# A fused two-block transformer step: one root for two norms, two projection tiles in turn, and retention in a new order

## The chip, the cores and the metric

The kernel runs on one core of one Trainium2 chip. The metric is the device time of one execution in microseconds, the median of several. All operands are float32 in HBM. The matrix products run on TensorE as three passes over split operands (below); vector work is on VectorE and ScalarE, a part of the splitting on GpSimd (POOL), and SyncE (SP) issues the DMAs.

## The reference, cut to what matters

Two blocks follow each other on 1024 tokens of width 1024. The first ends in a norm with gain g_final, the second begins with a norm with gain norm1 and a shift and scale from the condition c. A context of 256 tokens gets a norm of its own. The second block's projection has 29 tiles of 128 columns for gated linear attention and retention:

```python
def _rmsnorm(x, w):
    xf = x.astype(F32)
    y = xf * lax.rsqrt(jnp.mean(xf * xf, axis=-1, keepdims=True) + EPS)
    return (y * w).astype(x.dtype)

# end of the first block, start of the second
x  = _rmsnorm(x, g_final)
h  = _rmsnorm(x, norm1_w) * (1.0 + mod[:, 1]) + mod[:, 0]
hc = _rmsnorm(ctx, norm1_w) * (1.0 + mod_c[1]) + mod_c[0]
gq, gk, gv, gz, gg, rq, rk, rv, rg = split(h @ w_in)        # for the tokens; keys, values and gates of hc too

# retention, per head, forward and backward, chunk by chunk
scores = jnp.einsum('bhik,bhjk->bhij', qc, kc) * d_intra
o = jnp.einsum('bhij,bhjv->bhiv', scores, vc) + jnp.einsum('bhik,bhkv->bhiv', qc * q_decay, s)
s = c_decay * s + jnp.einsum('bhjk,bhjv->bhkv', kc * k_decay, vc)
o_r = _head_layernorm(o_rf + _flip(o_rb), ret_norm_w) * jax.nn.silu(rg)
```

Before this come the first block's four mixers, a feed forward and a gate; after it the output projection, a router and 16 experts.

## The kernel before

Activations lie transposed: 128 channels on the partitions, tokens along the free dimension, a tile of 8 x 1024 for the whole. Each operand of a large product is split into a high part (ScalarE, names ending in H) and a low part (VectorE or POOL, names ending in L). `gemm_steps` (line 258 on) then issues for each of 8 chunks k three matmuls, L264 to L266: high by high, low by high, high by low. The weights of tile n come into one of three buffers WR by a DMA of SP, ScalarE makes WH (L244), POOL makes WL (L252); WH and WL have two slots, and the slot of tile n is free for tile n + 2 when the last matmul of tile n is done.

The program is written by hand: for each engine there is one function that emits its instructions in order, and semaphores tie them together. `on.bank` makes the next user of a PSUM bank wait until the one before it has read it. `pe_program`, `act_program`, `dve_program`, `pool_program` and `sp_program` call the stages one after another. From the second norm to the retention, the projection of the second block (`in2_*`) is a filler: `Feed` on TensorE puts a given number of k steps between the instructions of the main stage, and notes how many units (one tile, one token segment) are then done; `Follow` on the other engines does the same units at the same point.

The second norm (`fin_*`): TensorE sums the squares over channels with a matmul by ones (`rstd_pe`, L281, banks 6 and 7; L1936, banks 4 and 5, for the squares with gain). ScalarE makes the first root as Exp(-0.5 Ln(mean + EPS)) (`rstd_act`, L293 and L298), VectorE squares it and multiplies it to the second sum (L1984, L1987), ScalarE makes the second root (L1952, L1954, once per token half), VectorE multiplies both (L1990). Then for 16 tiles of 512 tokens, 8 of the first half and 8 of the second: VectorE scales (L2004), ScalarE adds the shift and rounds to the high part (L1959), VectorE makes the low part (L1998), for which the first projection tile waits chunk by chunk. After these the squares of the context are made (L1967) and summed (L2012), one by one. A projection unit ends with a copy out of its bank: ScalarE for token segments 0 and 2 (L1880), VectorE for segment 1 (L1893), from bank 0 or 1.

Retention has four heads, h of 0 to 3, and two sets of buffers (`rmem[h % 2]`). On TensorE a head passes through: turning V (`ret_v_pe`, L2517) and K (`ret_k_pe` through `turn_pe`, L2127) to tokens on partitions, in groups of 4, 4 and 2 blocks through banks 6, 7, 6; scores (`ret_scores_pe`, L2532, banks 2 and 3); states (`ret_states_pe`, L2547); output (`ret_out_pe`, L2562 to L2564, banks 4 and 5); the root's sum (`ret_root_pe`, L281, banks 2 and 3). On VectorE: rope of K and Q (L2661, L2663, L2665), queries with decay (`ret_queries_dve`, L2736), mask on the scores (L2745), the chain of states (L2762, L2765), gate and norm (L2772, L2778, L2780). On ScalarE: decay tables (L2608, L2611), copies of V (L2133) and K (L2623, L2627), output copies (L2634, L2637), Tanh of the gate (L2642) and the root. The order in which the heads interleave is the order of the calls in `ret_pe_`, `ret_act_`, `ret_dve_` and `ret_sp`.

Of the kernel before, what the change touches and what calls it, by code (L numbers as in the profile page):

```python
# [132 lines left out]
def program(nc, I, out):  # L133
# [47 lines left out]
    def half(h):  # L181
        return slice(h * 512, h * 512 + 512)
# [1672 lines left out]

    def upto_v(*ms):

        return sum(len(s) for s in SEG[:1 + max(order2.index(m) for m in ms)])

    def in2_pe(e):  # L1860
        u = 0
        for n in range(29):
            for s, (a, b) in enumerate(SEG[n]):
                if s == 2:
                    e.wait_ge(*on("cx.lo", 7))
                e.wait_ge(*on.bank(s % 2, "in2", n, s))
                at_k = (lambda k: e.wait_ge(*on("fin.lo", s, k))) if n == 0 else None
                for _ in gemm_steps(e, N_IN2 + n, xs(S, XH2, XL2), a, b, s % 2, s == len(SEG[n]) - 1, at_k):
                    yield u
                u += 1  # L1870
                yield u

    def in2_act(e):
        for n in range(29):
            for s, (a, b) in enumerate(SEG[n]):
                if s != 1:
                    e.wait_ge(*on("gemm", N_IN2 + n, a))
                    if n >= 2:
                        e.wait_ge(*on("v", order2[n - 2]))
                    e.activation(stg2[:, n % 2 * S + a:n % 2 * S + b], bank[s % 2][:, 0:b - a], AF.Copy).then_inc(  # L1880
                        *i2_act.up("in2", n, s))
                if s == len(SEG[n]) - 1:
                    w_split_hi(e, N_IN2 + n + 2)
                yield

    def in2_dve(e):
        for n in range(29):
            for s, (a, b) in enumerate(SEG[n]):
                if s == 1:
                    e.wait_ge(*on("gemm", N_IN2 + n, a))  # L1890
                    if n >= 2:
                        e.wait_ge(*on("v", order2[n - 2]))
                    e.tensor_copy(stg2[:, n % 2 * S + a:n % 2 * S + b], bank[1][:, 0:b - a]).then_inc(  # L1893
                        *i2_dve.up("in2", n, s))
                yield

    def in2_pool(e):
        for n in range(29):
            for s in range(len(SEG[n])):
                if s == len(SEG[n]) - 1:  # L1900
                    w_split_lo(e, N_IN2 + n + 2)
                yield

    def in2_sp(e):
        for n in range(29):
            for s in range(len(SEG[n])):
                if s == len(SEG[n]) - 1:
                    w_load(e, N_IN2 + n + 3)
                    for k in range(len(SEG[n])):
                        e.wait_ge(*on("in2", n, k))  # L1910
                    size = SEG[n][-1][1]
                    e.dma_start(D_v[order2[n]][:, 0:size], stg2[:, n % 2 * S:n % 2 * S + size]).then_inc(
                        *d_v[n % 2].up("v", order2[n]))
                yield
# [16 lines left out]
    def fin_pe(e, st):  # L1931
        e.wait_ge(*on("ple.sum"))
        rstd_pe(e, acq, T, (6, 7), ("fin",))
        for h in range(2):
            e.wait_ge(*on.bank(4 + h, "fin.msq", h))
            e.matmul(bank[4 + h][:, :], ones, ac2[:, half(h)], start=True, stop=True).then_inc(*f_pe.up("fin.sum2", h))  # L1936
        st.until(2, "fin")
# [7 lines left out]

    def fin_act(e, st):
        A = f_act
        join(e, "ple")
        rstd_act(e, acq, 1024, T, (6, 7), ("fin",))
# [13 lines left out]
        for j in range(8):  # L1963
            if j > 1:
                e.wait_ge(*on("cx.add", j - 1))
# [11 lines left out]
    def fin_dve(e, st):  # L1977
# [30 lines left out]
        for j in range(1, 8):  # L2008
            e.wait_ge(*on("cx.sq", j))
            if j > 1:  # L2010
                e.wait_ge(*V.now)
# [1592 lines left out]
```

## Time and profile before

| | |
|---|---|
| time, median of 3 runs | 3753.26 us (3743.82 to 3764.45) |
| the profiled execution | 3762.52 us, span 3760.7 us |
| mean granted clock of TensorE | 0.975 |
| TensorE matmul busy | 3516.2 us (93%) |
| VectorE, ScalarE, POOL busy | 58%, 41%, 19% |
| second norm and first projection tiles | about 2162 to 2230 us of the span |
| retention | 2678.8 to 2790.8 us |
| experts | 2950 us to the end |

The span is the profiled core's time from its first instruction to its last. A share of busy time is an average over stages with different limits; what a stage is worth is read from its own waits. The granted clock is given as a share of full speed: 1.0 is 2.4 GHz and 0.5 is 1.2 GHz, and a value between is a mean over a stretch.

### The profile page before, as it was taken

To read this page: it belongs to the slowest core of one execution; us is meant where nothing else is said; L and a number is where in the kernel's file an instruction comes from. 1 tells how busy PE (TensorE), PEld (TensorE's weight loads), DVE (VectorE), ACT (ScalarE), POOL (GpSimd) and SP (SyncE) were. 2 spreads that over 40 slices of the span, in tenths; PEclk is the share of its full clock that TensorE was granted. 3 is DMA by queue.
4 is the path that set the end of the run, shared out by engine and by line. 5 is a ranking of instruction groups with operands and counts; after the bars stand their busy time and mean duration, and the time that the engine had idled before them with its cause. 6 is when DMAs were issued, how large, how long until landed. Compare 5 with 4: busy or idle time off the path is not lost. (4 is left out here: it accounts for less than half of the span.)

```text
span 3760.7 us, 45912 instructions
## 1 busy us (share of the span) xinstructions
PE 3516.2 (93%) x18441; PEld 2900.1 (77%) x18441; DVE 2170.5 (58%) x2868; ACT 1537.2 (41%) x1912; POOL 725.8 (19%) x330
## 2 busy tenths in 40 slices
PE   6999999999899999999999779999788799999996
PEld 4566777677687878888887657777666799999996
DVE  3334446545357444544425553636564899999996
ACT  3244442234212332222224342343453677766774
POOL 2111111112123122222222211111122112222210
PEclk9999999999999999999999999999989899999998
DMA  3111113143453234444311114131632899999996
GB/s 127 40 45 62 57 56 119 57 146 132 174 187 133 83 127 145 137 146 144 120 40 56 40 62 152 64 117 68 193 122 87 346 381 377 381 377 379 387 375 244
DMA packets 126692, 609.58 MB, mean 162 GB/s; under 512 B 14289, under 2 KB 15705, under 8 KB 101650
## 3 DMA queue, kind: packets, MB, share of 16 engines
q1 hardware_dynamic: 121730, 589.34, 42.8%
q0 software_dynamic: 4608, 16.78, 1.7%
q8 instruction: 148, 2.42, 0.3%
q10 hardware_dynamic: 144, 0.52, 0.0%
q14 instruction: 62, 0.51, 0.0%
HBM read 524.34 MB, written 82.22 MB: 161 GB/s over the span
## 5 line engine op out<-in xcount | busy, mean ns | idle before, releaser
L264 PE MATMUL bank<-XH,WH 128*128 128x512 f32 (+1 forms) x2568 | 1034.7, 403 | 63.7 <-DVE XL L1998 16.1
L265 PE MATMUL bank<-XL,WH 128*128 128x512 f32 (+1 forms) x2568 | 1003.9, 391 | 0.0
L266 PE MATMUL bank<-XH,WL 128*128 128x512 f32 (+1 forms) x2568 | 1001.0, 390 | 0.0
L252 POOL TENSOR_TENSOR WL<-WR,WH 128x1024 fp32r<-128x1024 f32 (+1 forms) x249 | 496.8, 1995 | 2205.5 <-ACT WH L244 2205.5
L264 PEld LDWEIGHTS bank<-XH,WH 128*128 128x128 f32 x2568 | 487.6, 190 | 211.8 <-issue 53.2
L266 PEld LDWEIGHTS bank<-XH,WL 128*128 128x128 f32 x2568 | 487.3, 190 | 105.6
L265 PEld LDWEIGHTS bank<-XL,WH 128*128 128x128 f32 x2568 | 488.5, 190 | 102.0 <-issue 6.5
L244 ACT ACTIVATE WH<-WR 128x1024 fp32r<-128x1024 f32 (+1 forms) x249 | 216.2, 869 | 598.4 <-PE bank L266 579.1
L3060 DVE TENSOR_TENSOR EL<-ER,EH 128x2816 fp32r<-128x2816 f32 x120 | 369.1, 3082 | 3.8 <-POOL warm L3303 3.8
L3055 ACT ACTIVATE EH<-ER 128x2816 fp32r<-128x2816 f32 x120 | 306.4, 2562 | 151.8 <-PE bank L3121 90.1
L3119 PE MATMUL bank<-EH,WH 128*128 128x352 f32 x1024 | 335.6, 328 | 1.5 <-DVE WL L3221 1.5
L3120 PE MATMUL bank<-EL,WH 128*128 128x352 f32 x1024 | 331.4, 324 | 0.0
L3121 PE MATMUL bank<-EH,WL 128*128 128x352 f32 x1024 | 330.9, 323 | 0.0
L264 PE MATMUL bank<-YH,WH 128*128 128x512 f32 x640 | 257.2, 402 | 19.9 <-POOL WL L252 19.9
L266 PE MATMUL bank<-YH,WL 128*128 128x512 f32 x640 | 255.0, 398 | 0.0
L265 PE MATMUL bank<-YL,WH 128*128 128x512 f32 x640 | 254.8, 398 | 0.0
L3311 POOL DMA_INDIRECT D_acc<-aq,iT x16 | 109.3, 6834 | 625.5 <-DVE aq L3235 625.5
L3129 PE MATMUL bank<-EH,HH 128*128 128x256 f32 x704 | 200.8, 285 | 0.0
L3130 PE MATMUL bank<-EL,HH 128*128 128x256 f32 x704 | 198.1, 281 | 0.0
L3131 PE MATMUL bank<-EH,HL 128*128 128x256 f32 x704 | 198.1, 281 | 0.0
L3119 PEld LDWEIGHTS bank<-EH,WH 128*128 128x128 f32 x1024 | 193.1, 189 | 1.8 <-DVE WL L3221 1.8
L3120 PEld LDWEIGHTS bank<-EL,WH 128*128 128x128 f32 x1024 | 193.3, 189 | 0.0
(516 smaller groups left out, 5051.2 us busy)
## 6 DMA issues: line engine op xcount, KB each, us to landing
ER<-in_wu_dram SPq DMA_DIRECT2D x48, 1408.0 KB, 9.1
ER<-in_wd_dram SPq DMA_DIRECT2D x40, 1408.0 KB, 10.0
aq<-in_w_ada_dram SPq DMA_DIRECT2D x96, 512.0 KB, 3.8
WR<-in_w_in_dram SPq DMA_DIRECT2D x89, 512.0 KB, 4.4
ER<-in_wg_dram SPq DMA_DIRECT2D x32, 1408.0 KB, 8.5
res<-in_wg_dram SPq DMA_DIRECT2D x16, 1408.0 KB, 8.3
res<-in_wu_dram SPq DMA_DIRECT2D x16, 1408.0 KB, 8.5
WR<-in_wg_dram SPq DMA_DIRECT2D x16, 1408.0 KB, 8.4
```

What stands on the lines that cost most here:

```text
L244: e.activation(hi, raw, AF.Copy).then_inc(*w_hi.up("w_hi", n))
L252: e.tensor_tensor(WL[:, n % 2 * 1024:n % 2 * 1024 + m], raw, hi.bitcast(F32), ALU.subtract).then_inc(*w_lo.up("w_lo", n))
L264: e.matmul(bank[bk][:, 0:b - a], whi, xhi, start=k == 0, stop=False)
L265: e.matmul(bank[bk][:, 0:b - a], whi, xlo, start=False, stop=False)
L266: mm = e.matmul(bank[bk][:, 0:b - a], wlo, xhi, start=False, stop=k == K - 1)
L3055: e.activation(eh(n), ER[n % NR], AF.Copy).then_inc(*x_act.up("e.hi", n))
L3060: e.tensor_tensor(EL[n % NR], ER[n % NR], eh(n).bitcast(F32), ALU.subtract).then_inc(*x_dve.up("e.lo", n))
L3119: e.matmul(bank[b][:, 0:QW], xh, eh(n, k * QW, k * QW + QW), start=k == 0, stop=False)
L3120: e.matmul(bank[b][:, 0:QW], xh, lo[:, k * QW:k * QW + QW], start=False, stop=False)
L3121: mm = e.matmul(bank[b][:, 0:QW], xl, eh(n, k * QW, k * QW + QW), start=False, stop=k == 7)
L3129: e.matmul(reg, hh, eh(n, k * 256, k * 256 + 256), start=k == 0, stop=False)
L3130: e.matmul(reg, hh, lo[:, k * 256:k * 256 + 256], start=False, stop=False)
```

## The change

Three parts. In the second norm, the two roots become one: with m the mean of the squares and m2 the mean of the squares with gain, the product of both roots is 1/sqrt(m2 + EPS m + EPS EPS). VectorE makes the argument from the two sums, and ScalarE takes Ln of both halves, then Exp of both halves. The first root alone, which the residual needs later, gets its Exp inside the loop over the 16 tiles. There too ScalarE makes the squares of the context, five instead of eight, and VectorE sums them afterwards in five steps.

The first two tiles of the projection are taken by token half in turn: tile 0 half 0, tile 1 half 0, tile 0 half 1, tile 1 half 1, with banks 2 and 3 for tile 1.

In retention the order of the calls changes on all four engines, K and V of heads 1 to 3 are turned through banks 2 and 3, the root's sum uses banks 4 and 5, and SP loads k2 before q2.

```diff
+    IN2_UNITS = [(n, k) for n in range(29) for k in range(len(SEG[n]))]
+    IN2_UNITS[:4] = [(0, 0), (1, 0), (0, 1), (1, 1)]
+    def in2_bank(n, s):
+        return s % 2 + 2 * (n == 1)
...
     def fin_act(e, st):
         A = f_act
         join(e, "ple")
-        rstd_act(e, acq, 1024, T, (6, 7), ("fin",))
+        e.wait_ge(*act_norm.now)
+        e.activation(warm, cn("eps"), AF.Ln).then_inc(*act_norm.up())
+        for h in range(2):
+            e.wait_ge(*on("fin", "sum", h))
+            e.activation(acq[:, half(h)], bank[6 + h][:, :], AF.Ln, scale=1.0 / 1024, bias=cn("eps")).then_inc(
+                *act_norm.up("fin", "mean", h))
         for h in range(2):
             e.wait_ge(*on("fin.msq", h))
-            e.activation(rr_[:, half(h)], rr_[:, half(h)], AF.Ln, bias=cn("eps")).then_inc(*A.up())
-            e.wait_ge(*A.now)
+            e.activation(rr_[:, half(h)], rr_[:, half(h)], AF.Ln).then_inc(*A.up("fin.ln", h))
+        for h in range(2):
+            e.wait_ge(*on("fin.ln", h))
             e.activation(rr_[:, half(h)], rr_[:, half(h)], AF.Exp, scale=-0.5).then_inc(*A.up("fin.rstd2", h))
...
+            if i in CX_SQ:
+                e.wait_ge(*on("cx"))
+                to, a, b = CX_SQ[i]
+                e.activation(to, cx[:, a:b], AF.Square).then_inc(*A.up("cx.sq", a))
+            if i in (13, 14):
+                e.wait_ge(*on("fin", "mean", i - 13))
+                e.activation(acq[:, half(i - 13)], acq[:, half(i - 13)], AF.Exp, scale=-0.5).then_inc(
+                    *act_norm.up("fin", "rstd", i - 13))
...
-            e.wait_ge(*on("fin", "rstd", h))
-            e.tensor_tensor(rq, acq[:, half(h)], acq[:, half(h)], ALU.mult).then_inc(*V.up())
+            e.wait_ge(*on("fin", "mean", h))
+            e.tensor_scalar(rq, bank[6 + h][:, :], EPS / 1024, EPS * EPS, ALU.mult, ALU.add).then_inc(*V.up())
             e.wait_ge(*on("fin.sum2", h))
             e.wait_ge(*V.now)
-            e.scalar_tensor_tensor(rq, bank[4 + h][:, :], 1.0 / 1024, rq, ALU.mult, ALU.mult).then_inc(*V.up("fin.msq", h))
-        for h in range(2):
-            e.wait_ge(*on("fin.rstd2", h))
-            e.tensor_tensor(ac2[:, half(h)], rr_[:, half(h)], acq[:, half(h)], ALU.mult).then_inc(*V.up())
+            e.scalar_tensor_tensor(rq, bank[4 + h][:, :], 1.0 / 1024, rq, ALU.mult, ALU.add).then_inc(*V.up("fin.msq", h))
...
     def ret_pe_(e):
         ret_scores_pe(e, 0)
+        ret_states_pe(e, 0)
         ret_v_pe(e, 1)
-        ret_states_pe(e, 0)
         ret_k_pe(e, 1)
-        ret_states_pe(e, 1)
         ret_out_pe(e, 0)
         ret_scores_pe(e, 1)
+        ret_states_pe(e, 1)
         ret_root_pe(e, 0)
         ret_k_pe(e, 2)
+        ret_out_pe(e, 1)
         ret_v_pe(e, 2)
-        ret_out_pe(e, 1)
+        ret_root_pe(e, 1)
...
+    def ret_turn_bank(h, c0):
+        return (2 if h else 6) + c0 // 4 % 2
```

ScalarE at the second norm, before; L1954 and L298 are Exp, L1952 and L293 Ln, L1959 the high parts:

```order
L293 ACTIVATE aq<-bank,con 128x512 x2
L298 ACT_TABLE_LOAD
L298 ACTIVATE aq<-aq 128x512 x2
L1952 ACT_TABLE_LOAD
L1952 ACTIVATE rr_<-rr_,con 128x512
L1954 ACT_TABLE_LOAD
L1954 ACTIVATE rr_<-rr_ 128x512
L1952 ACT_TABLE_LOAD
L1952 ACTIVATE rr_<-rr_,con 128x512
L1954 ACT_TABLE_LOAD
L1954 ACTIVATE rr_<-rr_ 128x512
L1959 ACTIVATE XH<-hb_,md 128x512 x16
```

The same place now; L1958 and L1962 are Ln, L1965 and L1978 Exp, L1970 the high parts, L1975 a square of the context:

```order
L1958 ACTIVATE aq<-bank,con 128x512 x2
L1962 ACTIVATE rr_<-rr_ 128x512 x2
L1965 ACT_TABLE_LOAD
L1965 ACTIVATE rr_<-rr_ 128x512 x2
L1970 ACTIVATE XH<-hb_,md 128x512 x4
L1975 ACTIVATE aq<-cx 128x512
```

Five table loads between the first Ln and the first high part have become one, and the squares stand between the high parts.

TensorE where the first half tile of the projection ends, before:

```order
L266 MATMUL bank0<-XH2,WL 128x512
L264 MATMUL bank1<-XH2,WH 128x512
L265 MATMUL bank1<-XL2,WH 128x512
L266 MATMUL bank1<-XH2,WL 128x512
L264 MATMUL bank1<-XH2,WH 128x512
```

The same place now:

```order
L266 MATMUL bank0<-XH2,WL 128x512
L264 MATMUL bank2<-XH2,WH 128x512
L265 MATMUL bank2<-XL2,WH 128x512
L266 MATMUL bank2<-XH2,WL 128x512
L264 MATMUL bank2<-XH2,WH 128x512
```

The matmuls into bank 1 (tile 0, second half) now follow those into bank 2 (tile 1, first half).

VectorE in retention, from the queries of head 0 on, before; L2661 to L2665 are a rope, L2745 the mask, L2762 and L2765 the states:

```order
L2736 TENSOR_TENSOR RM<-res,RM 128x1024 x2
L2745 SCALAR_TENSOR_TENSOR RM<-bank,RM 128x512 x2
L2661 TENSOR_TENSOR stg<-stg,res 128x1024
L2663 TENSOR_TENSOR RM<-RM,res 128x1024
L2665 TENSOR_TENSOR RM<-RM,stg 128x1024
L2661 TENSOR_TENSOR res<-res 128x1024
L2663 TENSOR_TENSOR res<-res 128x1024
L2665 TENSOR_TENSOR res<-res 128x1024
L2762 COPY RM<-bank 128x128
L2765 SCALAR_TENSOR_TENSOR RM<-RM,lg,bank 128x128 x3
L2762 COPY RM<-bank 128x128
L2765 SCALAR_TENSOR_TENSOR RM<-RM,lg,bank 128x128 x11
```

Now, behind the states of head 0 (L2798, L2801); L2695 to L2699 are a rope, L2770 queries, L2781 a mask:

```order
L2801 SCALAR_TENSOR_TENSOR RM<-RM,lg,bank 128x128 x11
L2695 TENSOR_TENSOR RM<-RM,res 128x1024
L2697 TENSOR_TENSOR RM<-RM,res 128x1024
L2699 TENSOR_TENSOR RM<-RM 128x1024
L2695 TENSOR_TENSOR res<-res 128x1024
L2697 TENSOR_TENSOR res<-res 128x1024
L2699 TENSOR_TENSOR res<-res 128x1024
L2770 TENSOR_TENSOR RM<-res,RM 128x1024 x2
L2781 SCALAR_TENSOR_TENSOR RM<-bank,RM 128x512 x2
```

The two ropes of head 2 (first K, in RM, then Q, in res) stand before the queries and the mask of head 1; before, they stood behind its mask and states.

## Rows read from the trace of the kernel before

**Rows 1.** The page, part 1: busy time, share of the span and instructions.
```profile
PE 3516.2 (93%) x18441; PEld 2900.1 (77%) x18441; DVE 2170.5 (58%) x2868; ACT 1537.2 (41%) x1912; POOL 725.8 (19%) x330
```
**Rows 2.** Waits of TensorE, 2155 to 2300: us in total, times, longest.
```profile
PE bank L264 <- DVE XL L1998: 16.1, 12, 12.2
...
PE bank L264 <- DVE stg L1893: 4.5, 1, 4.5
```
**Rows 3.** Timeline of the norm: start us, us, instruction [idle before].
```profile
2165.91 2.34 PE L1936 MATMUL bank<-aq,con 128*128 128x512 f32 x4
...
2166.15 0.69 ACT L293 ACTIVATE aq<-bank,con 128x512 f32<-128x512 f32 x1 [1.02 <-PE bank L281]
...
2169.61 0.69 DVE L1987 SCALAR_TENSOR_TENSOR rr_<-bank,rr_ 128x512 f32<-128x512 f32 x1
...
2175.32 1.28 ACT L1954 ACT_TABLE_LOAD   x1
...
2176.62 0.63 ACT L1954 ACTIVATE rr_<-rr_ 128x512 f32<-128x512 f32 x1
...
2178.01 1.41 DVE L2004 SCALAR_TENSOR_TENSOR hb_<-res,gc,aq 128x512 f32<-128x512 f32 x2
```
**Rows 4.** Timeline of the first projection tiles.
```profile
2199.79 0.50 PE L264 MATMUL bank<-XH,WH 128*128 128x512 f32 x1
...
2201.93 2.40 POOL L252 TENSOR_TENSOR WL<-WR,WH 128x1024 fp32r<-128x1024 f32 x1 [37.02 <-ACT WH L244]
...
2210.72 0.51 PE L264 MATMUL bank<-XH,WH 128*128 128x512 f32 x1 [4.46 <-DVE stg L1893]
...
2217.69 0.39 PE L266 MATMUL bank<-XH,WL 128*128 128x512 f32 x1
```
**Rows 5.** Stretches: us, busy (x) of PE, PEld, DVE, ACT, POOL, clock, DMA share.
```profile
2184.00:2200.00 16.00, 12.06 (x39) 6.04 (x38) 15.60 (x24) 8.80 (x13) 0.00 (x0) 1.00 0.00 0
...
2211.00:2214.00 3.00, 3.00 (x9) 2.26 (x9) 0.00 (x0) 0.00 (x0) 0.00 (x0) 0.53 0.82 266
...
2300.00:2500.00 200.00, 188.47 (x1231) 151.06 (x1231) 91.87 (x109) 72.41 (x93) 27.90 (x11) 0.98 0.26 93
```
**Rows 6.** Waits of TensorE in retention, 2660 to 2800.
```profile
PE bank L2127 <- DVE RM L2665: 10.1, 2, 8.2
```
**Rows 7.** Stretches of retention, columns as in rows 5.
```profile
2678.80:2783.70 104.90, 78.15 (x537) 69.06 (x535) 76.20 (x112) 53.51 (x103) 17.02 (x13) 0.87 0.37 121
...
2738.00:2746.00 8.00, 8.00 (x74) 8.00 (x74) 3.79 (x3) 5.29 (x10) 3.81 (x3) 1.00 0.17 63
```
**Rows 8.** Timeline of retention, one row for each kind of work.
```profile
2685.41 2.87 DVE L2736 TENSOR_TENSOR RM<-res,RM 128x1024 f32<-128x1024 f32 x2
...
2690.55 2.46 PE L2517 MATMUL bank<-con,RM 128*128 128x128 f32 x20
...
2729.66 2.42 ACT L2623 ACTIVATE RM<-bank,lg 128x512 f32<-128x512 f32 x4 [6.01 <-PE bank L2127]
...
2737.27 0.39 PE L2562 MATMUL bank<-RM 128*128 128x128 f32 x2
...
2742.63 4.18 PE L2547 MATMUL bank<-RM 128*128 128x128 f32 x36
...
2746.65 1.95 PE L2532 MATMUL bank<-res,RM 128*128 128x128 f32 x16
...
2747.82 1.51 DVE L2745 SCALAR_TENSOR_TENSOR RM<-bank,RM 128x512 f32<-128x512 f32 x2 [5.99 <-PE bank L2532]
...
2748.66 1.95 PE L281 MATMUL bank<-RM,con 128*128 128x512 f32 x4
...
2755.14 1.22 DVE L2661 TENSOR_TENSOR res<-res 128x1024 f32<-128x1024 f32 x1
...
2780.62 0.39 PE L2564 MATMUL bank<-RM 128*128 128x128 f32 x2
```
**Rows 9.** DMA issues of 2678 to 2740: KB each, median us to landing.
```profile
RM<-D_v SPq DMA_DIRECT2D x4, 640.0 KB, 7.6
```

More of the change, by code:

```diff
@@ L1862, in in2_pe @@
[L1862 to L1870, printed above, removed]
+        for u, (n, s) in enumerate(IN2_UNITS):
+            a, b = SEG[n][s]
+            if s == 2:
+                e.wait_ge(*on("cx.lo", 7))
+            e.wait_ge(*on.bank(in2_bank(n, s), "in2", n, s))
+            at_k = (lambda k: e.wait_ge(*on("fin.lo", s, k))) if n == 0 else None
+            for _ in gemm_steps(e, N_IN2 + n, xs(S, XH2, XL2), a, b, in2_bank(n, s), s == len(SEG[n]) - 1, at_k):
@@ L1871, in in2_pe @@
                 yield u
+            yield u + 1
     def in2_act(e):
[L1874 to L1884, printed above, removed]
@@ L1904, in in2_sp @@
-    def in2_sp(e):
[L1905 to L1914, printed above, removed]
+        for n, s in IN2_UNITS:
+            a, b = SEG[n][s]
+            if s != 1:
+                e.wait_ge(*on("gemm", N_IN2 + n, a))
+                if n >= 2:
+                    e.wait_ge(*on("v", order2[n - 2]))
+                e.activation(stg2[:, n % 2 * S + a:n % 2 * S + b], bank[in2_bank(n, s)][:, 0:b - a], AF.Copy).then_inc(
+                    *i2_act.up("in2", n, s))
+            if s == len(SEG[n]) - 1:
+                w_split_hi(e, N_IN2 + n + 2)
+            yield
@@ new lines, in in2_dve @@
+    def in2_dve(e):
+        for n, s in IN2_UNITS:
+            a, b = SEG[n][s]
+            if s == 1:
+                e.wait_ge(*on("gemm", N_IN2 + n, a))
+                if n >= 2:
+                    e.wait_ge(*on("v", order2[n - 2]))
+                e.tensor_copy(stg2[:, n % 2 * S + a:n % 2 * S + b], bank[in2_bank(n, s)][:, 0:b - a]).then_inc(
+                    *i2_dve.up("in2", n, s))
+            yield
+    def in2_pool(e):
+        for n, s in IN2_UNITS:
+            if s == len(SEG[n]) - 1:
+                w_split_lo(e, N_IN2 + n + 2)
+            yield
@@ L1936, in fin_pe @@
             e.matmul(bank[4 + h][:, :], ones, ac2[:, half(h)], start=True, stop=True).then_inc(*f_pe.up("fin.sum2", h))
+            on.bank(6 + h, "fin.msq", h)
         st.until(2, "fin")
@@ L2618, in ret_k_act @@
             e.wait_ge(*on("ret.kT", h, "T", c0))
-            b = bank[6 + c0 // 4 % 2]
+            b = bank[ret_turn_bank(h, c0)]
             for d in range(2):
```

110 lines of the change are left out of this document (60 added, 50 removed).

## The prediction, made before the changed kernel ran

> **What bounds the kernel now.** I read the busy table of the profile first: TensorE is busy 3516 of the 3760.7 us of the span [rows 1]. A change then pays only where TensorE waits, or runs at its lower clock. So I took the waits of TensorE next, stretch by stretch, for the two places that the diff touches.
>
> At the start of the second block TensorE waits 16.1 us for the low parts XL that VectorE makes, and 4.5 us for a copy out of bank 1 [rows 2], beside a shorter wait for the context's XL. The timeline shows where. The sums of squares come out of TensorE, then ScalarE and VectorE pass the ball for the two roots, and the first normalised tile starts on VectorE at 2178.01 [rows 3]. From there VectorE makes one XL with every two instructions, 24 instructions in 16 us, so one in 1.33 us [rows 5]. TensorE needs for the three matmuls that use it 0.69 us (from 2199.79 it ends the last three at 2200.5). It ends the second half of tile 0 at about 2200.5, does the first half of tile 1, stands until 2210.72 and ends tile 1 at 2218.1, 24 matmuls in 7.4 us [rows 4]. These hold a stretch at a granted clock of 0.53, the level of 1.2 GHz, right after the wait [rows 5].
>
> In the retention stage (2678.8 to 2783.7) TensorE's waits are many and small but for those on the rope of VectorE, 10.1 us with one of 8.2 [rows 6]. The mean granted clock is 0.87 there [rows 7], so some 27 us of 105 ran at 1.2 GHz, waits included (0.13 x 2 x 104.9).
>
> **The change, part A: one root.** Before, from the end of the last Ln of the first norm (2166.15 + 0.69 = 2166.84) to the first tile at 2178.01 stand 11.2 us [rows 3]. In it are five table loads of 1.28 us, of which ScalarE now needs one (the rows of its order, in the section on the change). New chain, with durations of rows 3: the square sum of half 0 leaves TensorE at about 2167.4 (second of four pieces of the row at 2165.91), that of half 1 at 2168.3. VectorE's two steps per half take 0.7 each; the first of half 0 runs at 2165.2, beside TensorE, then 2167.4 to 2168.1, then half 1 to 2169.5. Ln of half 1 ends at 2170.2, the load at 2171.5, Exp of half 0 at 2172.1. The first tile starts at 2172.2, so 5.8 us earlier. The product of the two roots (two VectorE steps) is gone as well; its only place on the chain is in these 11.2 us.
>
> The Trainium skill ("ScalarE: Activation LUTs", What ACT_TABLE_LOAD costs) charges 2.66 us for each switch, with a drain of 1.38 us. Here the load at 2175.32 takes 1.28 us and the ACTIVATE behind it starts 0.02 us after its end [rows 3], so the trace does not agree. By the page's figure four loads less would be worth 10.6 us instead of 5.1, which the 11.2 us with all their other work cannot hold.
>
> **Part B: two tiles in turn.** The steps are now tile 0 half 0, tile 1 half 0, tile 0 half 1, tile 1 half 1, in banks 0, 2, 1, 3. With D for the start on VectorE (now 2172.2): XL of half 0 is complete at D + 11.6. TensorE ends tile 0 half 0 at D + 12.3, tile 1 half 0 (8 x 0.69 = 5.5 us, nothing to wait for) at D + 17.8, tile 0 half 1 at D + 23.3 (the last XL is there at D + 22, just in time), tile 1 half 1 at D + 28.8 = 2201.0. Before, that point is 2218.1. A and B give 17.0 us; of that 5.8 is A, 5.5 the half tile that fits under VectorE's pace, 4.5 the wait for bank 1, and the rest mostly the lower clock after it.
>
> What hides the rest. The squares of the context move into ScalarE's loop: ScalarE is busy 8.8 of 16 us in that stretch [rows 5], 0.7 of each 1.33, and a square of 512 columns is an instruction like the Exp of 0.63 [rows 3], so its copies come hardly later, and VectorE has another tile to make before it wants one. VectorE's sums of the squares were 7 steps that alternated with ScalarE; now they are 5 of up to 0.7 with nothing between: 3 us, done at D + 25. The copy out of bank 1 is needed only at about D + 34. Next latest are the weights of tile 2: their slot is free at D + 23.3. Before, POOL had the low part of such a tile 3.8 us after the slot was free (2201.93 + 2.40, against 2200.5) [rows 4]. So it is ready at D + 27.1 for D + 28.8, a slack of 1.7 us; without it each us late costs one. The context chain behind stays as it is, since it begins after the same six units, and its wait with it. Bounds for A and B: 12 (weights 3 us late, and a wait of 2 us elsewhere) to 18.5 (clock at 2.4 GHz throughout).
>
> In between lies the gated linear attention with the projection as filler. TensorE is busy 188 of 200 us there [rows 5], its order is untouched, and nothing in it hangs on a time from outside, so it shifts as a whole.
>
> **Part C: retention.** I laid the new orders of the three engines side by side with durations of rows 8, at the higher clock. TensorE: turning V 2.4 (20 pieces); turning K half of it, 1.2 (10 pieces); scores 1.95; states 4.1; output 5.4 (2737.27 to 2742.63); root 2.0. VectorE: queries 2.8; one rope 3.5 (three like the row at 2755.14); mask and states together 7.3 (2747.82 to 2755.14), 1.4 of it the mask. ScalarE: the copies of K out of the banks 2.3, and 1.1 for the four short ones.
> - VectorE: queries end 2688.2, rope of q1 2691.7, mask 0 2693.2, rope of k1 2696.7, states 0 2702.6. TensorE has done states 0, V1 and K1 at about 2699.3 and waits 3.4 us for the states of VectorE. Output 0 runs 2702.7 to 2708.1.
> - Scores 1, states 1, root 0 follow without a wait, to 2716. The 8.2 us wait for the rope of k2 [rows 6] is gone: VectorE has it done at 2706.1. Its data are loaded ahead of q2 now, from 2690.8 on as before; such a load lands in 7.6 us [rows 9].
> - A new wait: the last two transposes of K2 need a bank that ScalarE empties only after root 0 (Ln and Exp of both halves and the load between [rows 3], decay tables 1.2, first copy 1.2), at about 2721.5. That is 4.6 us.
> - Output 1 2721.8 to 2727.2, V2, root 1, states 2, scores 2, V3 and K3 to 2742.4. Output 2 waits for the states on VectorE until 2744.4. States 3, root 2, scores 3 to 2758.1, output 3 to 2763.5.
>
> Before, output 3 ended at 2780.6 + 0.2 [rows 8], so 17.2 us earlier at the higher clock. The tail behind it (last root, gate, store) is the same work. Charge for the clock: a wait of 4.5 us was followed by a stretch at 0.53 [rows 5] that cost 1.9 us (7.4 for 5.5). The waits of 3.4 and 4.6 us, and that before K0, may each cost that much, 5.7 in all; some of it falls into waits on VectorE. I take 4.7 off: part C is worth 12.5 us. Bounds: 5 (the low clock as often as before, and another wait like that on K2) and 17.2.
>
> The Trainium skill ("TensorE: Matmul & The Clock Gate", Part 1) says that the array falls back to 1.2 GHz when it idles and comes back after sustained work, whatever the instructions are. The trace agrees (0.53 behind the wait, 1.00 from 2738 on in retention [rows 5, 7]). It speaks against this change where one wait becomes two shorter ones.
>
> One more thing comes nearer: the six loads of the heads for the output projection are released by scores 3. Now that is at 2758, and they are needed at about 2774. The nearest row is 7.6 us for a load that shares the queue with others [rows 9], so they stay hidden.
>
> **Sum.** 17.0 + 12.5 = 29.5 us. The profiled execution took 3762.52 us in all for its span of 3760.7; it would come to 3733. It lies 9.3 us over the median of the three runs, 3753.26, so I forecast 3724 us.
>
> **Rivals.**
> - Retention returns nothing: waits on ScalarE behind each root, as on K2, four times 4.6 us, and lower clock after each eat the 17 us. For it: the bank turn of K and V has to pass through ScalarE in order. Against: only K2 stands directly behind a root in ScalarE's order. Time 3753.3 - 17.0 = 3736.
> - The turn of two tiles gives nothing, since TensorE waits for tile 2's weights or a bank instead; only the root stays. Against: the slack of 1.6 us and two more banks. Time 3753.3 - 5.8 - 12.5 = 3735.
> - The clock stays up all through retention and no new wait appears beyond those listed: 17.0 + 17.2 = 34.2, time 3719.
> - Slower: TensorE's clock. If the shorter waits hold the granted clock at 1.2 GHz all through retention, its 68 us of work (4 heads x 17) take 68 more, of which 9 fill the new waits. Against the 34.2 us that the change brings at the higher clock this is a loss of 25, 3778. It decides from about 43 of the 68 us at 1.2 GHz on. Against it: before, the clock was back at 1.00 from 2738 to 2746, in the middle of the stage and 10 us after its longest wait [rows 6, 7].
>
> **Chances.** Forecast 0.60, retention nothing 0.17, turn nothing 0.08, clock all up 0.11, slower 0.04. What a measurement of this kernel can tell from no change is about 0.5%, or 18.8 us. Below 3734.5 lie the forecast, the best case and some of the two middle ones, which sit on the bound: faster 0.76, same 0.20, slower 0.04. The range takes the bounds, 17 to 35.7 us, and the 6 us by which a median of such runs may lie elsewhere (the three runs differ by 20.6): 3711 to 3741.
>
> **What would show it.** Right if ScalarE has one table load between the first Ln and the first XH copy; if the first XH matmul of the block starts 6 us nearer to the sums; if TensorE has no wait for L1893's successor and 48 matmuls more by D + 29; if the wait for the rope of k2 is gone, with 3 to 4 us before output 0 and 4 to 5 us in K2 in its place; and if the stage up to the end of output 3 takes 90 us and not 102. Wrong if the stretch from 2230 to 2678 does not shift rigidly, or a new wait above 5 us stands in either place.

## The result and the profile after

The changed kernel takes 3719.35 us (median of 5 runs, 3714.7 to 3727.58), the kernel before beside it 3754.1 us (5 runs, 3743.82 to 3764.45). The ratio is 0.9912, 95% interval 0.9898 to 0.9926, so about 33 us less. Forecast were 3724 us and a range of 3711 to 3741. The profiled execution of the changed kernel is its longest of the five, 3727.58 us with a span of 3725.8, and its mean granted clock 0.976.

The busy time of TensorE, part 1 of the page, answers to [rows 1]: 12.5 of the 35 us that the two spans differ by are TensorE's own time, the rest is waits. Of the 12.5 us 10.8 lie ahead of the norm (2066.8 and 2056.0 us busy up to its first sum), in stages that the change doesn't touch; more on them at the end of this section.

```profile
PE 3503.7 (94%) x18441; PEld 2900.5 (78%) x18441; DVE 2167.7 (58%) x2864; ACT 1530.9 (41%) x1905; POOL 728.3 (20%) x330
```

The waits of TensorE from 2155 to 2300 (in total, times, longest) answer to [rows 2]: the wait for the first XL is 6.3 us instead of 12.2, and that for bank 1 is gone. The wait for the context's XL (L2039) was there before too.

```profile
PE bank L264 <- DVE XL L2007: 7.2, 4, 6.3
PE bank L264 <- DVE XL L2039: 2.5, 1, 2.5
PE bank L264 <- ACT stg L1883: 2.0, 4, 0.6
```

The timeline of the norm (start, duration, instruction, idle before) answers to [rows 3]. Behind the last Ln of the means (2155.91) follow the argument, one Ln a half, one table load, the two Exps and the first tile. From the end of that Ln to the first tile 5.0 us pass, where it was 11.2.

```profile
2155.91 0.69 ACT L1958 ACTIVATE aq<-bank,con 128x512 f32<-128x512 f32 x1 [1.02 <-PE bank L281]
...
2158.32 0.69 DVE L2000 SCALAR_TENSOR_TENSOR rr_<-bank,rr_ 128x512 f32<-128x512 f32 x1
2159.04 0.63 ACT L1962 ACTIVATE rr_<-rr_ 128x512 f32<-128x512 f32 x1 [0.76 <-DVE rr_ L2000]
2159.69 1.28 ACT L1965 ACT_TABLE_LOAD   x1
2160.98 1.15 ACT L1965 ACTIVATE rr_<-rr_ 128x512 f32<-128x512 f32 x2
2161.64 1.41 DVE L2015 SCALAR_TENSOR_TENSOR hb_<-res,gc,rr_ 128x512 f32<-128x512 f32 x2 [2.64 <-ACT rr_ L1965]
2164.08 0.77 PE L264 MATMUL bank<-XH,WH 128*128 128x512 f32 x1 [6.34 <-DVE XL L2007]
...
2186.42 2.41 POOL L252 TENSOR_TENSOR WL<-WR,WH 128x1024 fp32r<-128x1024 f32 x1 [31.74 <-ACT WH L244]
```

The last row is GpSimd's low part of tile 2's weights, ready at 2188.8. TensorE starts tile 2 at 2190.57, without a wait, so the slack is 1.7 us.

The waits of TensorE in retention, 2640 to 2790, answer to [rows 6]. None is left for the rope of head 2.

```profile
PE bank L2546 <- ACT RM L2657: 7.2, 4, 4.7
PE bank L2587 <- DVE RM L2801: 2.6, 2, 1.7
PE bank L2536 <- ACT RM L2645: 2.2, 1, 2.2
PE bank L2546 <- DVE RM L2699: 1.9, 1, 1.9
```

The timeline of TensorE there answers to [rows 8]: head 0's scores, the start of output 0, the scores of head 1 behind it, the last two transposes of K2, and the last root's sum.

```profile
2660.89 3.62 PE L2557 MATMUL bank<-res,RM 128*128 128x128 f32 x16
...
2675.68 0.77 PE L2587 MATMUL bank<-RM 128*128 128x128 f32 x2 [1.69 <-DVE RM L2801]
...
2683.99 1.95 PE L2557 MATMUL bank<-res,RM 128*128 128x128 f32 x16
...
2697.23 0.69 PE L2546 MATMUL bank<-con,RM 128*128 128x128 f32 x2 [4.68 <-ACT RM L2657]
...
2743.63 1.98 PE L281 MATMUL bank<-RM,con 128*128 128x512 f32 x4 [0.69 <-ACT RM L2668]
```

Four stretches, columns as in [rows 5]: retention up to the end of output 3, and outputs 0, 1 and 2 alone. The same work, 5.4 us at the full clock, took 8.31, 7.50 and 7.06 us, at granted clocks of 0.64, 0.70 and 0.76. The mean of the stage is 0.87, as before [rows 7].

```profile
2651.13:2742.95 91.82, 76.18 (x533) 70.23 (x531) 76.02 (x111) 51.31 (x99) 18.60 (x13) 0.87 0.40 123
...
2675.68:2683.99 8.31, 8.31 (x49) 8.31 (x50) 8.24 (x7) 2.25 (x7) 3.53 (x3) 0.64 0.01 4
2697.71:2705.21 7.50, 7.50 (x50) 7.50 (x50) 7.43 (x7) 2.73 (x8) 1.49 (x2) 0.70 0.41 142
2722.15:2729.21 7.06, 7.06 (x48) 7.06 (x49) 5.57 (x5) 1.90 (x6) 0.00 (x0) 0.76 0.10 39
```

One difference lies in code that the change doesn't touch. In the feed-forward, some 700 us ahead of it, the two profiled executions keep a different pace at the same granted clock of 1.00: 431 matmuls in 100 us before, 439 after. By the start of the norm this has put the profile of after 10.2 us ahead (2152.10 against 2162.33).

```profile
1420.00:1520.00 100.00, 100.00 (x431) 80.98 (x430) 49.27 (x108) 20.24 (x30) 22.60 (x14) 1.00 0.48 151
```
```profile
1420.00:1520.00 100.00, 100.00 (x439) 82.05 (x438) 50.29 (x113) 20.67 (x30) 23.36 (x15) 1.00 0.46 150
```

### The profile page after: what moved, and what is told of

Its sections match the earlier page's. It is cut to its first block and busy times, and to the rows that moved or that the text cites. A ratio compares the mean times of both kernels' runs of the same rounds, so it can differ in the third digit from the quotient of the medians.

```text
span 3725.8 us, 45897 instructions
## 1 busy us (share of the span) xinstructions
PE 3503.7 (94%) x18441; PEld 2900.5 (78%) x18441; DVE 2167.7 (58%) x2864; ACT 1530.9 (41%) x1905; POOL 728.3 (20%) x330
```

## The experiments

Each kernel was timed several times beside the kernel before; a ratio is to that. The table has, from the one profiled execution of each, in us: from the norm's first sum matmul to the first matmul of tile 2; from there to the first turn of V of head 0, called V0 below (the attention lies in between); from V0 to the sum of the last root; and the pace of the feed-forward (matmuls in 1420 to 1520).

| kernel | sum to tile 2 | tile 2 to V0 | V0 to last root | pace | ratio, 95% interval |
|---|---|---|---|---|---|
| before | 55.59 | 460.86 | 102.91 | 431 | |
| e4, before again | 55.58 | 460.31 | 103.03 | 438 | 0.9998, 0.9986 to 1.0011 |
| e1, root only | 43.20 | 459.36 | 105.91 | 439 | 0.9964, 0.9952 to 0.9977 |
| e2, turn only | 47.18 | 462.0 | 102.94 | 438 | 0.9973, 0.9961 to 0.9986 |
| e3, retention only | 56.03 | 461.18 | 92.40 | 430 | 0.9955, 0.9939 to 0.9971 |
| e12, root and turn | 38.78 | 457.03 | 103.13 | 439 | 0.9959, 0.9945 to 0.9974 |
| after | 38.47 | 460.56 | 92.50 | 439 | 0.9912, 0.9898 to 0.9926 |
| e11, after again | 38.54 | 456.80 | 90.22 | 438 | 0.9904, 0.9887 to 0.9920 |
| e5, squares behind | 38.75 | 457.52 | 92.44 | 438 | 0.9909, 0.9889 to 0.9929 |
| e6, K2 in another bank | 38.71 | 456.61 | 86.07 | 438 | 0.9895, 0.9875 to 0.9915 |
| e7, split later | 38.54 | 456.48 | 90.44 | 439 | 0.9914, 0.9895 to 0.9934 |
| e8, fill at head 0 | 38.48 | 456.88 | 90.09 | 430 | 0.9912, 0.9892 to 0.9932 |
| e9, e6 and e7 | 38.53 | 457.47 | 85.57 | 438 | 0.9899, 0.9883 to 0.9916 |
| e10, e9 with fill | 38.57 | 456.75 | 83.35 | 438 | 0.9886, 0.9869 to 0.9902 |

The three columns of times are of one execution each, and code that kernels share takes up to 4 us more in one than in another. A difference of that size between two rows shows nothing by itself.

**e1, part A alone.** One root, and the squares of the context in the loop.

```diff
 before.py
-            e.activation(rr_[:, half(h)], rr_[:, half(h)], AF.Ln, bias=cn("eps")).then_inc(*A.up())
+            e.activation(rr_[:, half(h)], rr_[:, half(h)], AF.Ln).then_inc(*A.up("fin.ln", h))
+            if i in CX_SQ:
...
```

> The kernel before with the one root and the context's squares inside ScalarE's loop, the projection tiles in their old order, retention as before. Theory (the parts add up, each by its own wait): the first tile starts 6.1 us nearer to the sums (11.2 us shrink to 5.1 after the first Ln), and the 4.5 us wait for bank 1 goes with the 1.9 us of low clock behind it, since VectorE sums the squares in 3 us and no longer in step with ScalarE: 12.5 us from the sums' matmul to the end of tile 1, ratio about 0.9967. Rival (only the root counts, the wait for bank 1 was removed by the new banks and not by the squares): 6 us, ratio 0.9984, and a wait for bank 1 of 3 us or more stays.

Measured: 3739.93 us against 3754.19. From the sum to the first tile it is 9.62 us instead of 15.68, and to tile 2 12.4 us less. Beside the root, the wait for bank 1 is gone: VectorE's copy out of that bank no longer stands behind seven sums that alternate with ScalarE's squares. So the theory held and the rival is out. In retention, where e1 has the code of before, its profile took 105.91 us, 3 more, with the same waits for the rope (10.1 us, one of 8.2) but a granted clock of 0.84 instead of e4's 0.87. TensorE's waits from 2148 to 2200:

```profile
PE bank L264 <- DVE XL L2006: 9.7, 11, 6.3
PE bank L281 <- DVE aq L1812: 7.5, 1, 7.5
```

**e2, part B alone.** The two first tiles in turn; root and squares as before.

```diff
 before.py
+    IN2_UNITS[:4] = [(0, 0), (1, 0), (0, 1), (1, 1)]
+        return s % 2 + 2 * (n == 1)
```

> The kernel before with the first two projection tiles in turn and banks 2 and 3, nothing else. Theory: the half tile that fits under VectorE's pace (5.5 us), the bank wait and its low clock (6.4 us) are gained, but ScalarE makes the squares of the context, in step with VectorE, ahead of the weights of tile 2, which come at 34 us after the first tile's start where TensorE wants them at 28.8: a wait of 5 to 6 us in front of tile 2 and low clock behind it, so 4 us net, ratio 0.9989. Rival (weights in time): 11.9 us, ratio 0.9968.

Measured: 3742.5 us against 3754.19. To tile 2 it is 8.4 us less. The four units end 11.0 us earlier (at 44.75 behind the sum), and then TensorE waits 2.43 us for the low part of tile 2's weights. The wait of the theory is there, but half as long as the 5 to 6 us expected, so the gain is twice the 4 us. By the time it is 11.7 us, with an interval (5.3 to 14.6 us) that leaves out the 4 us and holds the rival's 11.9; it is the wait in the trace that excludes the rival. ScalarE had come to the high part of the weights only behind the eight squares, of which all but the first two wait for a sum of VectorE; they take 6.2 us (2188.30 to 2194.48):

```profile
2194.06 0.42 ACT L1968 ACTIVATE rc_<-cx 128x256 f32<-128x256 f32 x1 [0.49 <-DVE rc_ L2013]
2194.39 1.04 ACT L244 ACTIVATE WH<-WR 128x1024 fp32r<-128x1024 f32 x1
...
2198.00 0.47 PE L264 MATMUL bank<-XH,WH 128*128 128x512 f32 x1 [2.43 <-POOL WL L252]
```

**e3, part C alone.** The orders of retention, its banks and the order of two loads.

```diff
 before.py
-            ret_load_sp(e, h + 2, "q", "qs", "k", "ks")
+            ret_load_sp(e, h + 2, *(("q", "qs", "k", "ks") if h else ("k", "ks", "q", "qs")))
...
+        return (2 if h else 6) + c0 // 4 % 2
```

> The kernel before with the new order, banks and loads of retention, nothing else. Theory: the stage from the first turn of V to the last root's sum takes 92.5 us as in the changed kernel and not 102.9, 10.4 us, ratio 0.9972, with the wait of 4.7 us in the turn of K2 there. Rival (part of the 34.8 us by which the medians differ comes from something that the parts share, as the place of the code): the stage gains 10.4 us in the trace but the time moves by more than 13 us.

Measured: 3736.08 us against 3754.19, and 10.5 us less in retention, the 10.4 of the changed kernel. That is the theory's number for the stage, but the time did what the rival says: it moved by 18.1 us, with an interval of 10.9 to 22.9. Only the 12.7 us by which e11's retention is below 102.91 lie in it. The two profiles, before and e3, both of the slower pace, differ by 9.6 us in span (3760.7 and 3751.1): 10.5 in retention and -0.9 elsewhere. But this profiled execution of e3, 3752.93 us, is the second longest of its nine, and seven lie between 3728.5 and 3738.2. Where those are shorter no profile shows. For the rival's reason, that the parts share something, there is no sign: e12's 17.7 and e3's 18.1 add up to 35.8 us, and the changed kernel has 34.8.

**e4, the kernel before with a comment.**

> The kernel before, unchanged. Both profiled executions ran the same code up to the second norm, but the feed forward's matmuls stood 0.2327 us apart in the one of before and 0.2283 us in the one of after, at a granted clock of 1.00 in both, which is 10.2 us at the second norm. Theory (the pace differs from execution to execution): this one shows either pace, ratio 1.000 within 0.002. Rival (the pace belongs to the kernel's code): it shows 0.2327 us again, and every changed kernel 0.2283.

Measured: 3753.19 us against 3754.19. Its profile has the faster pace (438) and a span of 3751.4, 9.3 less than the 3760.7 of the profile before. So the pace belongs to the execution. The e3 and e8 profiles, of changed code, have the slower one.

**e12, parts A and B.** Both edits in the kernel before, and retention as it was.

```diff
 before.py
+    IN2_UNITS[:4] = [(0, 0), (1, 0), (0, 1), (1, 1)]
...
-            e.activation(rr_[:, half(h)], rr_[:, half(h)], AF.Ln, bias=cn("eps")).then_inc(*A.up())
+            e.activation(rr_[:, half(h)], rr_[:, half(h)], AF.Ln).then_inc(*A.up("fin.ln", h))
```

> The kernel before with the one root and the turn of the two first tiles (parts A and B), and without the retention's new sequences (part C). Theory (the parts lie apart in time and add, and the join of A and B gives 17.1 us, less than 12.4 and 8.4 of each alone since both take the wait for bank 1 away): from the norm's sum to tile 2 38.5 us, as in the changed kernel, retention 103 us, as before, and the time 17 to 21 us below before (3733 to 3738), the rest to the changed kernel being 10.4 to 12.3 us of part C. Rival (the stretch between tile 2 and the retention, which took 459.4 to 462.0 us in five kernels without both parts and 456.5 to 457.5 in seven of the eight with all, owes its 3.5 us to part C, or to chance): it takes 459 to 462 us here; if it belongs to A and B together, 456.5 to 457.5, and the time is 20 to 24 us below before.

Measured: 3733.91 us against 3751.64, 17.7 less. To tile 2 it is 16.8 us less, in retention nothing (103.13). The stretch to V0 is 457.03, as the rival has it if its 3.5 us belong to A and B together; the time goes with the theory (17 to 21 us), though its interval, 9.8 to 20.6, just takes in the rival's 20 to 24.

**e5, the changed kernel with the squares behind the loop.**

```diff
 after.py
-            if i in CX_SQ:
-                e.wait_ge(*on("cx"))
...
         st.upto("fin")
+        e.wait_ge(*on("cx"))
+        for i in CX_SQ:
```

> The changed kernel, with the five Squares of the context behind the loop over the sixteen tiles again, all else as in the changed kernel. Theory (the squares' move is what keeps a wait for tile 2's weights away once the first tile is early and two tiles run in turn): behind the four units PE now waits for the low half of tile 2's weights, which GpSimd forms from the rounded half that ScalarE writes behind the squares (five Squares at 0.6 us or less are about 2.7 us). In the kernel with the turn alone that wait was 2.4 us. Here 2 to 4 us of wait in front of tile 2, from the norm's sum to tile 2 about 41 to 42 us instead of 38.5, and the whole 2 to 4 us over the changed kernel. Rival (weights have room to spare in the join, since the root comes 6 us earlier for ScalarE too): no wait, 38.5 us, the same time within 1 us. In both the context's own sums are late by at most 2 us and nothing waits for them.

Measured: 3717.59 us, 38.75 us to tile 2 and no wait. The theory fell. Five squares in a row, each of up to 512 columns, take ScalarE 2.3 us, and the weights are split right behind them (columns as in the other timelines), ready at 2184.0 for 2185.15:

```profile
2178.03 1.15 ACT L1980 ACTIVATE aq<-cx 128x512 f32<-128x512 f32 x2
2179.07 0.93 ACT L1980 ACTIVATE rc_<-cx 128x512 f32<-128x512 f32 x2
2179.90 0.41 ACT L1980 ACTIVATE stg<-cx 128x256 f32<-128x256 f32 x1
2180.21 1.05 ACT L244 ACTIVATE WH<-WR 128x1024 fp32r<-128x1024 f32 x1
...
2181.33 2.68 POOL L252 TENSOR_TENSOR WL<-WR,WH 128x1024 fp32r<-128x1024 f32 x1 [32.35 <-ACT WH L244]
```

Here five squares take 2.3 us, where e2's eight took 6.2, and the 3.9 us between them are more than e2's wait of 2.43. So it was the alternation of eight squares with the sums that made the weights late in e2, and that the squares stand in the loop is worth nothing here.

**e6, head 2's last key transposes in bank 6.**

```diff
 after.py
+    def ret_k_bank(h, c0):
+        return 6 if (h, c0) == (2, 8) else ret_turn_bank(h, c0)
```

> The changed kernel, with the third group of transposes of head 2's key in bank 6 instead of bank 2, so that it no longer waits until ScalarE has read bank 2 behind head 0's root. Theory (the wait of 4.7 us is on the path, and the clock's fall behind it too): the wait in front of those two transposes goes, output 1 begins at once and about half of it at the full clock instead of at half; 4 to 7 us less from the first value turn to the last root (92.5 us in the changed kernel, 86 to 88.5 here), and the whole 4 to 7 us shorter. Rival (what ScalarE and VectorE still have to do for heads 1 and 2 is late as well): PE waits as long a little later, for the value's copies, for root 1's squares or for the keys of head 2 in front of the states; 91 to 92.5 us, the whole as the changed kernel.

Measured: 3711.27 us, and 86.07 us in retention: 6.4 less than after, 4.2 less than e11, as the theory has it. The ten transposes of K2 run in one, and output 1 follows after 1.05 us:

```profile
2683.39 1.25 PE L2549 MATMUL bank<-con,RM 128*128 128x128 f32 x10
2685.70 0.46 PE L2590 MATMUL bank<-RM 128*128 128x128 f32 x2 [1.05 <-DVE RM L2804]
```

**e7, the last weight split behind the masks.**

```diff
 after.py
-            if s == len(SEG[n]) - 1:
+            if s == len(SEG[n]) - 1 and n < 28:
...
+            if h == 1:
+                w_split_lo(e, N_IN2 + 30)
```

> The changed kernel, with the last weight split of the in2 phase (GpSimd, 2.89 us, needed only by out2 some 100 us later) behind the masks of heads 0 and 1. Theory (VectorE's multiplication of key 0 took 3.37 us where the same operation takes 1.22 elsewhere, and its excess of 2.15 us coincides with that split): the multiplication takes 1.2 to 1.5 us, key 0 is ready about 2 us earlier, the wait of 1.9 us in front of its transposes goes, and the stage is 2 to 3 us shorter (92.5 to about 90). Rival A (the excess came from something else, such as the transfers that land meanwhile): it takes 3.4 us as before and nothing changes. Rival B (the masks slow VectorE as the split did): the excess moves or shrinks to less than 1 us, and under 1 us is won.

In the changed kernel the split (first row) covers VectorE's multiplication of key 0 (second row); in e7 that takes 1.48 us and the wait of 1.9 us is gone.

```profile
2652.46 2.89 POOL L252 TENSOR_TENSOR WL<-WR,WH 128x1024 fp32r<-128x1024 f32 x1 [14.39 <-ACT WH L244]
...
2653.07 3.37 DVE L2697 TENSOR_TENSOR RM<-RM,res 128x1024 f32<-128x1024 f32 x1
```

But the price has only moved to the operation that now runs beside the split (e7: the multiplication of key 0, the split, and the last step of the rope of head 1's query):

```profile
2645.43 1.48 DVE L2699 TENSOR_TENSOR RM<-RM,res 128x1024 f32<-128x1024 f32 x1
...
2652.77 3.33 POOL L252 TENSOR_TENSOR WL<-WR,WH 128x1024 fp32r<-128x1024 f32 x1
...
2653.92 3.26 DVE L2701 TENSOR_TENSOR res<-res 128x1024 f32<-128x1024 f32 x1
```

Output 0 starts 24.57 us behind V0, in the changed kernel 24.55. The 90.44 us look like a gain against 92.50, but e11 has 90.22 without the edit. The time, 3719.84, says nothing won. That is rival B as to the size, though not because the masks slow VectorE as much: the excess didn't shrink, it changed its victim.

**e8, matmuls of constants in the first two waits.** Their output is read by nothing.

```diff
 after.py
         ret_v_pe(e, 0)
+        fill_pe(e, 2)
         ret_k_pe(e, 0)
...
+            e.matmul(bank[B_S[0][0]][:, 0:128], ones, ident, start=True, stop=True)
```

> The changed kernel, with eight 128x128 matmuls of constants (1.95 us at the full clock, their output is read by nothing) in each of the two first waits of the retention: in front of the last group of head 0's value turn (wait 2.2 us) and behind it, in front of the key's transposes (wait 1.9 us). Theory (the clock falls behind those waits and head 0's transposes, scores and the first states run at half speed for it): the granted clock of the stretch from 5 to 13 us behind the stage's start goes from 0.61 to above 0.9, the scores of head 0 take 1.95 instead of 3.62 us, and 2 to 3.5 us are won if nothing else is late. Rival (VectorE's masks and states are late anyway): the clock stays up, but PE waits as much longer in front of the states' outputs or of head 1's key, and under 1 us is won.

The clock stayed up. The stretch from 4.68 to 15.21 us behind V0, first in the changed kernel, then in e8:

```profile
2655.81:2666.34 10.53, 8.05 (x45) 7.50 (x44) 10.46 (x10) 3.83 (x9) 7.75 (x6) 0.68 0.39 147
```
```profile
2664.52:2675.05 10.53, 9.35 (x80) 8.77 (x79) 10.46 (x10) 3.83 (x9) 7.77 (x6) 1.00 0.65 231
```

Output 0 starts at 24.57 us again, now behind a wait of 3.39, and retention takes 90.09 us (e11: 90.22); the time is 3720.63. So it is the rival. VectorE is busy 10.46 of 10.53 us in both.

**e9, e6 and e7 together.**

```diff
 after.py
+        return 6 if (h, c0) == (2, 8) else ret_turn_bank(h, c0)
...
+                w_split_lo(e, N_IN2 + 30)
```

> The changed kernel with both edits of the two runs before: head 2's third group of key transposes in bank 6, and GpSimd's last weight split behind the masks of heads 0 and 1. Theory (two waits at places 30 us apart on one path, 6.4 and 2.1 us alone): both gains stand, 8 to 8.5 us, 84 us from the first value turn to the last root (92.5 in the changed kernel), the whole about 3711 us against the changed kernel's 3719. Rival (the work of VectorE between them sets a pace of its own, and takes back what the first one gives): only the larger of the two stands, 86 us.

Measured: 3714.9 us (3712.55 to 3718.49), 85.57 us, where e6 alone has 86.07. Of the 8 to 8.5 us expected only e6's part stands, as the rival has it.

**e10, the edits of e9, with fill before V0's last group and before output 0.**

```diff
 after.py
         ret_k_pe(e, 1)
+        fill_pe(e, 12)
         ret_out_pe(e, 0)
```

> Both edits, and beside them matmuls of constants whose output nothing reads in two waits: eight in front of the last group of head 0's value turn (2.2 us of wait), and twelve (2.9 us) in front of output 0, where PE waits 3.4 us for the last state of head 0. Theory (each of these waits lets the clock fall for some 5 us of work behind it): the granted clock of the 6 us of output 0's work goes from 0.5 to 0.9 or more, 2 us are won there and up to 1 us at head 0's key and scores; 81 to 82.5 us. Rival (VectorE is busy without a gap until norm 0 and sets when scores 1 and states 1 are used; a faster output 0 only waits longer there): at most 1 us less than with the two edits alone, 83 to 84 us.

Measured: 3710.75 us (3709.17 to 3711.73), 83.35 us. Output 0 took 5.36 us at a clock of 1.00 (stretch of e10, then the row of the fill ahead of it):

```profile
2670.18:2675.54 5.36, 5.36 (x50) 5.36 (x49) 5.29 (x6) 1.08 (x2) 0.00 (x0) 1.00 0.01 3
```
```profile
2665.88 4.47 PE L2537 MATMUL bank<-con 128*128 128x128 f32 x24
```

The fill took 4.5 us instead of 2.9, so output 0 started 0.57 us late, and before output 1 TensorE waits 1.84 us for ScalarE's root 0, where e9 waits 0.57 us for VectorE. In retention 2.2 us are won against e9, of which the output itself has 2.8 (8.2 us in e9). So the gain is the theory's 2 to 3, and more than the rival's 1; the 83.35 us stand above the theory's 81 to 82.5 because e9, its base, came out at 85.57 and not at 84. One profile of each has to carry this. All runs of e10 lie below all of e9 and of e11, which were timed beside it; from e6 (3711.27 us, ratio 0.9895) it can't be told apart.

**e11, the changed kernel with a comment.**

> The changed kernel again, with a comment added and nothing else, as the yardstick beside the other two. If what its profile showed 3 to 5 us longer than those of four kernels with the same code there (the stretch from the third tile of in2 to the retention, and the experts) belongs to the execution and not to the code, this profile shows 456.5 to 461.5 us for the first and 968 to 971.5 us for the second again, and 92.5 us within 0.3 for the retention, which does not vary so. The time 3717 to 3721 us. If it belonged to the code, both would stand at 460.6 and 971.4.

Measured: 3719.64 us (3713.02 to 3721.83). The first part held, 456.80 us and 968.8 us (from the first matmul of the output projection to the end); that retention doesn't vary was wrong, it took 90.22 us at a mean clock of 0.92. Here head 0's scores took 2.48 us instead of 3.62, the wait before output 0 is 3.26, and outputs 0 and 1 ran 6.89 and 6.75 us at 0.78, as output 2 did (6.92 us):

```profile
2658.30 2.48 PE L2557 MATMUL bank<-res,RM 128*128 128x128 f32 x16
...
2673.41 0.77 PE L2587 MATMUL bank<-RM 128*128 128x128 f32 x2 [3.26 <-DVE RM L2801]
```
```profile
2673.41:2680.30 6.89, 6.89 (x48) 6.89 (x49) 6.82 (x6) 1.09 (x2) 1.19 (x1) 0.78 0.05 17
2694.03:2700.78 6.75, 6.75 (x49) 6.75 (x49) 6.68 (x6) 2.73 (x8) 1.49 (x2) 0.78 0.46 158
```

## Why the prediction was right, and where it was off

**Part A.** Forecast 5.8 us to the first tile, measured 6.1 (15.68 to 9.54). The chain is the one that was added up.

**Parts A and B.** Forecast 17.0 us to tile 2, measured 17.1 (55.59 to 38.47), and 16.8 in e12. Tile 1 half 1 was put at D + 28.8 and ended at D + 28.9; the slack of tile 2's weights was put at 1.7 us and is 1.7. What the prediction listed as separate terms is not separable, though. Part A alone gives 12.4 us and part B alone 8.4: the wait of 4.5 us for bank 1, and the low clock behind it, goes with either, and B alone pays 2.4 us for the weights.

**The stretch between.** "It shifts as a whole" is the step that failed, by the prediction's own sign of being wrong. The stretch took 459.4 to 462.0 us in the five kernels without A and B together, and 456.5 to 457.5 in eight of the nine with both; the profile of after, with 460.56, is the exception. Some 3.5 us were won in most executions that no term had. The rows of the whole stretch, e4 and then e11, show what they are. TensorE has the same matmuls to do (2691 and 2692 records) and is busy 434.8 us in the one and 432.0 in the other, at a mean granted clock of 0.98 and 0.99. These are 2.8 us; the other 0.7 are a wait for a load of the keys, 1.1 us in e4 and 0.4 in e11. The profile of after has 435.1 us, 0.98 and 1.1 us, so it is as e4 is.

```profile
2208.45:2668.76 460.31, 434.81 (x2691) 347.95 (x2690) 221.10 (x283) 156.24 (x202) 71.41 (x27) 0.98 0.33 112
```
```profile
2192.05:2648.85 456.80, 432.01 (x2692) 345.86 (x2691) 221.09 (x283) 156.29 (x202) 71.44 (x27) 0.99 0.33 113
```

Why the clock holds better in most executions when the stretch starts some 17 us earlier, and didn't in the one of after, is open. So is whether it is the change at all: eight of nine against none of five speaks for it, but each kernel has one profile only, and that doesn't prove it.

**Part C.** Forecast 12.5 us, measured 10.4 to 10.5 in three profiles of four with this code as it is (after, e3, e5) and 12.7 in the fourth (e11), all from the 102.91 of before. The large waits are those that were laid out: none on the rope of k2, 4.7 us in K2 (forecast 4.6), and 3.3 before output 0 in e11 (forecast 3.4); the one before output 2 is 0.9 us and was put at 2.0. In the three profiles the charge for the clock was mis-sized. It stood at 4.7 us; in the profile of after outputs 0, 1 and 2 took 2.9, 2.1 and 1.7 us more than the 5.4 at the full clock, 6.7 together, and the start of output 0 was 0.65 us late. That is the whole distance between the 84.7 us that the layout gave for the end of output 3, counted from V0, and the 91.8 measured (0.65 + 6.7 = 7.3 against 7.1). In e11 outputs 0, 1 and 2 took 1.5, 1.4 and 1.5 us more, 4.4 together, so there the charge was right. e6 shows both parts of the price of the K2 wait: without it output 1 starts 3.7 us earlier than in e11 and takes 5.4 us instead of 6.75, and retention is 4.2 us shorter (6.4 against after, whose output 0 was slower too).

The output 0 rows show the other thing that the layout had right: VectorE's chain sets it. It started 24.55 to 24.57 us behind V0 in after, e3, e5 to e9 and e11, whatever TensorE did until then (e10, with its fill too long, 25.13). So the slow scores of head 0 (3.62 us instead of 1.95) didn't move that start. Whether they cost something behind it is not settled: in the three profiles with 3.62 us (after, e3, e5) output 0 took 8.3 us and retention 92.4 to 92.5; with scores of 1.95 to 2.88 us (e11, e7, e8) it took 6.8 to 7.0 and retention 90.1 to 90.4; but e9 had scores of 1.95 us and an output 0 of 8.2.

**The sum.** e4 and e11 have the same pace, and their spans differ by 32.8 us (3751.4 and 3718.6). It is 17.0 up to tile 2, 3.5 in the stretch between, 12.8 in retention, 0.1 behind it, and -0.6 ahead of the norm. Forecast were 29.5. The 3.5 us are the missing term. That the spans of before and after differ by 34.9 us, as the medians do (34.8), is luck of two executions: 10.2 us of it lie ahead of the norm, 17.1 up to tile 2, 0.3 in the stretch between and 10.4 in retention, and behind the last root the profile of after is 3.2 us longer than that of before (982.2 and 979.0 us; 978.7 to 979.6 in the twelve others). The 10 us by which the two first profiles differed ahead of the norm are the execution's pace and no part of the change, as taking both against medians had rightly left out.

**The rivals.** Retention gave its gain, the turn gave its part, and the clock did not stay up. The rival of the clock at 1.2 GHz all through is excluded by 0.87.

**Sums.** Two small ones in the prediction don't close: the bounds give 3711.6 to 3742.3 us where the range says 3711 to 3741, and the slack of the weights is 1.7 us in one place and 1.6 in another. Neither changes a reading.

## What to carry to other kernels

Where two engines pass a stage between them, lay out both orders from the durations in the trace: the two largest waits came out within 0.2 us, a third at 0.9 instead of 2.0, and the start that the slower engine sets within 0.7. Charge the lower clock separately for each wait of TensorE, here 1.4 to 2.9 us for an output that follows one, and only where TensorE and not its supplier sets the end. Before paying to remove an excess (a slow VectorE operation, a slow clock) look for the engine that starts the next fixed point; e7 and e8 removed real losses and won nothing, while e6 took a wait of 4.7 us out of the path, and retention became 4.2 us or more shorter. And take a second profile of both kernels before reading differences of 3 us between two: what looks like 2.1 us won by e7 against one profile of the changed kernel is nothing against the other.

## What the hardware showed unexpectedly

At a granted clock of 1.00 in both, the feed-forward ran at 430 or 431 matmuls in 100 us in three profiles and at 438 or 439 in the eleven others, with the kernel before and with changed ones; the norm's first sum starts at 2162.2 to 2164.5 us in the three and at 2146.4 to 2154.1 in the others. VectorE's 128x1024 operation of two SBUF inputs takes 1.22 us alone, 1.36 to 1.48 beside GpSimd's masks, and 3.26 to 3.37 beside its 128x1024 subtraction of 2.9 to 3.3 us. Where the granted clock falls and comes back differs between executions of one program by enough to move the retention by 2.3 us (92.50 at a mean of 0.87 and 90.22 at 0.92; with the orders of before 103.03 at 0.87 and, in e1, 105.91 at 0.84).
